# Forgetting attention rebuilt on transposed scores, with rounded high and low parts, inside a two-block kernel

## The reference, cut to what matters

```python
proj = einsum('bld,de->ble', rmsnorm(x), w_in)      # z_ssm, xbc, dt, q, k, v, f, z_att, g_ssm, g_att
log_f = log_sigmoid(f_raw + fgate_b)                # 16 heads
fcum = cumsum(log_f, axis=-1)
for blk in range(8):                                # 128 queries each, head width 64
    s = einsum('bhqd,bhkd->bhqk', q[q0:q1], k[:q1]) * 64 ** -0.5
    s = s + fcum[q0:q1, None] - fcum[None, :q1]
    s = where(kpos <= qpos, s, -inf)
    prob = softmax(s, axis=-1)
    o[q0:q1] = einsum('bhqk,bhkd->bhqd', prob, v[:q1])
y_att = o * silu(z_att)
merged = sigmoid(g_ssm) * (y_ssm @ w_branch_ssm) + sigmoid(g_att) * (y_att @ w_branch_att)
out = x + rmsnorm(merged @ w_out)
```

## Time and profile before

| what | value |
|---|---|
| runs shown | 3496.93 us median of 3 (3496.38 to 3499.29) |
| profiled execution, its time / its span | 3497.23 us / 3495.4 us |
| PE, DVE, ACT, POOL busy over the span | 86%, 60%, 39%, 9% |
[...]

### The profile page before, as it was taken

One profiled execution on the slowest core, in us unless ns is written; L12 is line 12 of the kernel. 1 busy time (PEld: TensorE's weight loads), 2 busy tenths in 40 slices (PEclk: granted clock), 3 DMA queues, 4 the chain that ended last, 5 costly groups with the idle time before them and its releaser, 6 DMA issues. The chain is left out here.

```text
span 3495.4 us, 39550 instructions
## 1 busy us (share of the span) xinstructions
PE 2989.5 (86%) x14122; PEld 2406.6 (69%) x14122; DVE 2101.0 (60%) x2553; ACT 1376.2 (39%) x1961; POOL 298.9 (9%) x215
## 2 busy tenths in 40 slices
PE   6977886999988999998967994978799859999992
PEld 5855665888876777786756871656587848888881
DVE  4773544343325666334544789878345469999993
ACT  3342333323332333332243342333332237777770
POOL 0001300000000000000000000000000014443430
PEclk9986898999998999999988996989899769999996
DMA  3100010111221110111121110000111449999995
GB/s 85 49 14 1 0 43 24 48 49 49 97 78 38 25 25 13 49 49 37 43 72 44 49 32 0 1 25 25 43 49 43 172 153 394 383 376 375 376 351 225
DMA packets 169958, 349.60 MB, mean 100 GB/s; under 512 B 33313, under 2 KB 33313, under 8 KB 169824
## 3 DMA queue, kind: packets, MB, share of 16 engines
q1 hardware_dynamic: 158496, 322.66, 27.0%
q0 software_dynamic: 9216, 16.80, 1.3%
q10 hardware_dynamic: 2112, 8.39, 0.7%
HBM read 326.76 MB, written 37.81 MB: 104 GB/s over the span
## 5 line engine op out<-in xcount | busy, mean ns | idle before, releaser
L2069 DVE TENSOR_TENSOR ex_w<-ex_raw,ex_w 128x2048 fp32r<-128x2048 f32 x192 | 436.1, 2290 | 49.6 <-ACT ex_w L2016 47.2
L2016 ACT ACTIVATE ex_w<-ex_raw 128x2048 fp32r<-128x2048 f32 x192 | 364.0, 1916 | 89.9 <-DMA ex_raw<-in_w_down_e 32.4
L1946 PE MATMUL ps<-ex_w,ex_xT 128*128 128x512 f32 x1536 | 366.2, 395 | 5.3 <-DVE ex_xT L2078 5.1
L1946 PEld LDWEIGHTS ps<-ex_w,ex_xT 128*128 128x128 f32 x1536 | 287.2, 189 | 67.5 <-DVE ex_xT L2078 6.4
L729 DVE TENSOR_TENSOR bs_t<-arena,bs_t 128x1024 fp32r<-128x1024 f32 x80 | 98.1, 1226 | 283.3 <-ACT bs_t L693 283.3
L609 DVE SCALAR_TENSOR_TENSOR arena<-arena,small 128x1023 f32<-128x1023 f32 (+9 forms) x168 | 213.7, 1272 | 4.3
L672 PE MATMUL ps<-bs_t,bs_w 128*128 128x512 f32 x512 | 201.4, 393 | 11.1 <-DVE bs_w L732 9.0
L693 ACT ACTIVATE bs_t<-arena 128x1024 fp32r<-128x1024 f32 x80 | 84.9, 1061 | 298.2 <-PE ps L674 269.4
L673 PE MATMUL ps<-bs_t,bs_w 128*128 128x512 f32 x512 | 200.5, 392 | 0.0
L674 PE MATMUL ps<-bs_t,bs_w 128*128 128x512 f32 x512 | 200.4, 391 | 0.0
L1946 PE MATMUL ps<-ex_w,ex_hT 128*128 128x512 f32 x768 | 186.0, 399 | 7.3 <-DVE ex_hT L2089 7.3
(11 more groups left out here) (369 smaller groups left out, 6832.0 us busy)
## 6 DMA issues: line engine op xcount, KB each, us to landing
ex_raw<-in_w_gate_e SPq DMA_DIRECT2D x64, 1024.0 KB, 13.2
ex_raw<-in_w_up_e SPq DMA_DIRECT2D x64, 1024.0 KB, 13.1
ex_raw<-in_w_down_e SPq DMA_DIRECT2D x64, 1024.0 KB, 13.5
arena<-in_w_in SPq DMA_DIRECT2D x108, 512.0 KB, 3.7
arena<-in_x SPq DMA_DIRECT2D x4, 2048.0 KB, 11.5
arena<-in_w_out SPq DMA_DIRECT2D x16, 512.0 KB, 3.7
arena<-expert_out SPq DMA_DIRECT2D x8, 1024.0 KB, 12.2
arena<-in_w_branch_ssm SPq DMA_DIRECT2D x8, 512.0 KB, 3.7
```

The costliest lines, as they stand in the source:

```text
L1946: mm = nc.tensor.matmul(out, l, r, start=(k == 0 and n == 0), stop=(k == kc - 1 and n == 2))
L2016: nc.scalar.activation(half_of(part[m][0], h), raw[m][:, h * W // 2: (h + 1) * W // 2], ACT.Identity).then_inc(high[m], 1)
L2069: V.tensor_tensor(half_of(part[m][1], h), raw[m][:, h * W // 2: (h + 1) * W // 2], half_of(as_f32(part[m][0]), h), ALU.subtract)\
```

## The change

Scores are made transposed: keys in partitions, up to 512 queries in columns. A head has 12 tiles (g, j): 512 queries g by 128 keys j, cut at the diagonal to 512, 384, 256 or 128 columns, 4608 columns in all. All large products are fp32r.

- q, k and v leave the dense phase as high and low parts (kinds `split`, `split_T`): ACT rounds each bank into one tile, DVE subtracts into another, and ACT issues 8 DMAs for each q or k job and 2 for each v job, into DRAM tensors of packed rows: `qa`, `ka` (128 rows) and `qb`, `kb` (66 and 67 rows). The v jobs now come last.
- Per head PE makes a first approximation of the scores in the old orientation, only for the row maxima (`top`, L1032, L1035); DVE reduces them (L1166); PE turns the 128x8 maxima, ACT rounds them, and SP sends them to DRAM and back as one row of `b` (L959, L962).
- Per tile: two products make the score (L1060, L1062, mask L1065), ACT makes the exponential and a rounded copy, GpSimd subtracts for the low part, and PE makes three products with the values (L1084 to L1089). Ones stand beside the 64 columns of values, so that the sum of a column of probabilities comes out in another row of the same bank.
- The sums go to DRAM and back as 128x8 (L967, L969), are inverted, go to DRAM and back spread over 64 partitions (L974, L979), and DVE multiplies a pair of heads by them (L1185).
- The output is feature-major, so "ya" goes away; `za` and `ba` become one phase of eight jobs, with the gate multiplied on DVE beside the g_att jobs (`gate_heads`).
- `phase_decays` rounds the sums in two more DVE instructions, stores two rows, and fills rows of ones.

```diff
@@ phase_decays
+    run_high, run_low = (r[0:HEADS, :] for r in c.rounded("dec_run", 5, 2 * SEQ + 112, SEQ))
+    unit = c.ones[0:HEADS, :].unsqueeze(1).to_broadcast([HEADS, SEQ // P, P])
+            for t, row in (("qa", HD), ("qa", HD + 1), ("kb", HD + 2)):
+                sp.dma_start(att[t][:, row, :].rearrange("h (k n) -> h k n", n=P), unit)\
+                    .then_inc(stored, 16)
             sp.wait_ge(step, RUN_DONE)
-            sp.dma_start(fcum_dram, run).then_inc(stored, 16)
-            sp.wait_ge(stored, 16)
+            for row, part in ((HD, run_high), (HD + 1, run_low)):
-            st.done(V.tensor_tensor_scan(run, one_row, fT, 0.0, ALU.mult, ALU.add))
+            st.then_wait(V.tensor_tensor_scan(run, one_row, fT, 0.0, ALU.mult, ALU.add))
+            st.then_wait(V.tensor_copy(run_high, run))
+            st.done(V.tensor_tensor(run_low, run, run_high.bitcast(F32), ALU.subtract))
...
@@ phase_dense
+            def high_evict(j):
+                for m in splits:
+                    if m < j and jobs[m][3] is jobs[j][3]:
+                        act.wait_ge(kept[m], stores[m])
+                for t in range(TT):
+                    act.wait_ge(product, TT * j + t + 1)
+                    nc.scalar.activation(jobs[j][3][0][:, t * BANK:(t + 1) * BANK], c.ps[:, t, :],
+                                         ACT.Identity, scale=jobs[j][6]).then_inc(halved, 1)
+                for m in splits:
+                    if n - 1 == last[m] + 1 or (n == NS and last[m] >= NS - 1):
+                        if n == NS and last[m] >= NS - 1:
+                            high_evict(m)
+                        act.wait_ge(by_vec, before(m + 1, False))
+                        stores[m] = jobs[m][5](act, kept[m], jobs[m][3])
+                    elif j in splits:
+                        dve.wait_ge(halved, TT * splits.index(j) + t + 1)
+                        part = slice(t * BANK, (t + 1) * BANK)
+                        x = V.scalar_tensor_tensor(out=dst[1][:, part], in0=src, scalar=jobs[j][6],
+                                                   in1=dst[0][:, part].bitcast(F32), op0=ALU.mult,
+                                                   op1=ALU.subtract)
...
@@ phase_forget_attention, SP, GpSimd and PE of the new one
+            for h in range(HEADS):
+                if h + 2 < HEADS:
+                    load_a(h + 2)
+                if h + 1 < HEADS:
+                    load_b(h + 1)
+                if h:
+                    keep_sums(h - 1)
+                if h + 1 < HEADS:
+                    move_shift(h + 1)
+                if h % 2 == 0 and h + 2 < HEADS:
+                    load_v(h // 2 + 1)
+                if h:
+                    spread_inverse(h - 1)
...
+                    pool.wait_ge(rounded, x + 1)
+                    if x >= 4:
+                        pool.wait_ge(valued, x - 3)
+                    nc.gpsimd.tensor_tensor(low[x % 4][:, 0:w], prob[x % 3][:, 0:w],
+                                            f32(high[x % 4][:, 0:w]), ALU.subtract).then_inc(lowered, 1)
...
+                    pe.wait_ge(b_in[h % 2], 32 * (h // 2 + 1))
+                    pe.wait_ge(shift_in, 16 * (h + 1))
+                if x >= 3:
+                    pe.wait_ge(exped, x - 2)
+                bank = c.ps[:, S_BANK[x % 3], :]
+                (qa, ka), (qb, kb) = a_of[h % 3], b_of[h % 2]
+                diag = j >= 4 * g
+                nc.tensor.matmul(bank[:, 0:w], ka[:, ks], qa[:, qs], start=True, stop=False,
+                                 skip_group_check=True)
+                mm = nc.tensor.matmul(bank[:, 0:w], kb[0:BR, ks], qb[0:BR, qs], start=False,
+                                      stop=not diag, skip_group_check=True)
+                if diag:
+                    mm = nc.tensor.matmul(bank[:, 0:P], c.identb[:], c.maskTb[:, 0, :], start=False,
+                                          stop=True, skip_group_check=True)
...
+                pe.wait_ge(rounded, x + 1)
+                nc.tensor.matmul(to, vl_, high[x % 4][:, 0:w], start=(j == 0), stop=False,
+                                 skip_group_check=True)
+                nc.tensor.matmul(to, vh_, high[x % 4][:, 0:w], start=False, stop=False,
+                                 skip_group_check=True)
+                pe.wait_ge(lowered, x + 1)
+                nc.tensor.matmul(to, vh_, low[x % 4][:, 0:w], start=False, stop=(j == 4 * g + 3),
+                                 skip_group_check=True).then_inc(valued, 1)
+                    score(h, i)
+                    if h + 1 < HEADS and i < TT - EARLY:
+                        top(h + 1, i + EARLY)
+                    if h + 1 < HEADS and i == TT - EARLY + 1:
+                        turn_shift(h + 1)
+                    if h + 2 < HEADS and i >= NT - EARLY:
+                        top(h + 2, i - (NT - EARLY))
+                    if i >= 3:
+                        values(h, i - 3)
...
@@ phase_forget_attention, DVE of the new one
+                if h >= 3 and h % 2:
+                    norm((h - 3) // 2)
+                for t in range(EARLY, TT):
+                    if h + 1 < HEADS:
+                        maxima(h + 1, t)
+                if h:
+                    take(h - 1, 1)
+                take(h, 0)
+                if h:
+                    invert(h - 1)
+                for t in range(EARLY):
+                    if h + 2 < HEADS:
+                        maxima(h + 2, t)
+            take(HEADS - 1, 1)
+            invert(HEADS - 1)
...
@@ _build
+                    + [(T(R(0)), wcol(w_in, (C_Q, C_K)[n // 2], n % 2), "split_T", staged[n % 2], None,
+                        store_heads(n % 2, n // 2), (float(HD) ** -0.5, 1.0)[n // 2]) for n in range(4)]
+                    + [(T(R(0)), wcol(w_in, C_V, n), "split", staged[n % 2], None, store_values(n), 1.0)
+                       for n in range(2)], 5)
+        phase_forget_attention(c, att, sums, inverse, shifts)
+        def gate_heads(n, tapped, by_act, by_vec, moved):
+
+            for x in range(2 * (n - 2 * KC), 2 * (n - 2 * KC) + 2):
+                if 0 <= x < KC:
+                    if x == 0:
+                        nc.vector.wait_ge(by_act, 2 * TT)
+                    yk = T(R(4))[:, x, :]
+                    nc.vector.tensor_tensor(yk, yk, T(R(1))[:, x, :], ALU.mult).then_inc(tapped, 1)
+
+        phase_dense(c, "za", [(T(R(0)), wcol(w_in, C_ZA, n), "act_T", wide(1, n), ACT.Silu)
                               for n in range(2)]
                     + [(T(R(0)), wcol(w_in, C_GA, n), "act_T", wide(3, n), ACT.Sigmoid)
-                       for n in range(2)], 5)
-        phase_turn(c, "ya", R(4), R(5), gate=R(1))
-        phase_dense(c, "ba", [(T(R(5)), wcol(a["w_branch_att"][0], 0, n), "muladd_T", wide(2, n),
-                               wide(3, n)) for n in range(2)]
+                       for n in range(2)]
+                    + [(T(R(4)), wcol(a["w_branch_att"][0], 0, n), "muladd_T", wide(2, n),
+                        wide(3, n)) for n in range(2)]
                     + [(T(R(2)), wcol(a["w_out"][0], 0, n), "act", half(R(3), n), ACT.Identity)
-                       for n in range(2)], 1, made_by={2: 0, 3: 0})
+                       for n in range(2)], 5, aside=gate_heads, made_by={6: 4, 7: 4}, gated_by=(4, 5))
```

More of the change, by code:

```diff
@@ new lines, in phase_forget_attention @@
+    NT = 3 * TT // 2
+    TILES = [(g, j) for g in range(2) for j in range(4 * g + 4)]
+    assert len(TILES) == NT
+    BR, EARLY = HD + 3, 5
+    a_of = [c.named(f"fa_a{s}", 1, s * 2 * SEQ, SEQ, F32R, 2) for s in range(3)]
+    b_of = [c.named(f"fa_b{s}", 3, s * 2 * SEQ, SEQ, F32R, 2) for s in range(2)]
+    rinv = [c.named(f"fa_rinv{s}", 1, 6 * SEQ + s * SEQ, SEQ) for s in range(2)]
+    prob = [c.named(f"fa_p{s}", 3, 4 * SEQ + s * BANK, BANK) for s in range(3)]
+    high = [c.named(f"fa_ph{s}", 3, 4 * SEQ + (3 + s) * BANK, BANK, F32R) for s in range(4)]
@@ new lines, in phase_forget_attention @@
+    shift = c.named("fa_shift", 3, 4 * SEQ + 7 * BANK, 2 * P, F32R)
+    VW = 3 * HD
+    vh, vl = ([c.named(f"fa_v{n}{s}", 5, (2 * s + n) * TT * VW, TT * VW, F32R)
+               .rearrange("p (t n) -> p t n", t=TT) for s in range(2)] for n in range(2))
+    low = [c.named(f"fa_pl{s}", 5, 4 * TT * VW + s * BANK, BANK, F32R) for s in range(4)]
+    out = c.at(4, 0, REGION)
+    negmax = [c.small[:, SEQ + TT * s:SEQ + TT * (s + 1)] for s in range(2)]
+    inv = [c.small[:, SEQ + 16 + TT * s:SEQ + 16 + TT * (s + 1)] for s in range(2)]
@@ L899, in phase_forget_attention @@
-        turned = S("turned")
-        placed = S("placed")
-        summed = S("summed")
-        stored = S("stored")
+        a_in, b_in = [S(f"a_in{s}") for s in range(3)], [S(f"b_in{s}") for s in range(2)]
+        v_in = [S(f"v_in{s}") for s in range(2)]
+        filled = S("filled")
+        topped, negated = S("topped"), S("negated")
+        shift_turned, shifted = S("shift_turned"), S("shifted")
```

(80 more changed lines are left out.)

349 lines of the change are left out of this document (197 added, 152 removed).

## The result

The changed kernel takes 3710.57 us (median of four runs, 3687.82 to 3711.99) against 3496.65 for the kernel before on the same chip: ratio 1.0604, interval 1.0565 to 1.0642. I had forecast 3452 us and faster; it is 214 us slower.

The account below looks back on a forecast made before the run. The prediction took TensorE to bound the attention stage, at about 348 us. From 3497.2 us it subtracted 22.3 (attention and its earlier start) and 25.4 (joined phases) and added 2.5 (`phase_decays`): 3452 us, range 3404 to 3492.

Parts of the forecast that it names:

- the pricing of the dense phases: In `bs`, the added stores and their issues cost nothing; up to 8 us allowed in the range.
- rival C: In the attention, SP's small hops take 4.5 us instead of 1.9 behind loads: 3525 us, slower than before; chance 0.08.
- start of bs: Before the dense phase, two more operations in `phase_decays` on the path to the store add 2.5 us.
- to the attention: Between `bs` and the attention, the first product comes 2.3 us earlier, with the clearing gone from the path.
- attention: From the attention's first product to `za`: 328.5 us against 348.5 before, 20 less.
- za and ba joined: Joining the two phases removes TensorE's gap between them except a 0.3 us boundary: 25.4 us less.
- The late inverse: In odd heads, the inverse returns late behind value loads: 5.4 us lost in each of 7 pairs, 38 us.
- The start of the attention: Eight blocks of maxima, turn, rounding and the way out and back put the first score 14 us after the first product.
- A head: One attention head takes 16.6 us: 14.8 of TensorE products and masks, plus 0.5, 0.8 and 0.5.
- rival B: In the attention, narrow products and slower tile hand-overs make a head 18.4 us: 3481 us; chance 0.17.
- Narrow products: Twelve 128-column products a head cost between 0.117 us and 0.234 us (two records) each; 0.5 us a head taken.
- what would show it wrong: Attention signs: odd and even heads equal, `shift_in` ending TensorE's wait, ACT mostly waiting for GpSimd, or heads under 15.5 us.

Follow-up runs that it names:

- e9: Only groups of stores from ScalarE's queue, back to back, the rest of the computation left out; the four 62-row stores took 83.7 us together.
- e1: The changed kernel with only its 62-row stores cut into 48 and 14 rows: 3585.96 us, ratio to the kernel before 1.0254.
- e5: e3 with the stores of a query or key job issued in pairs behind five steps of the next job: 3453.09 us, ratio to the kernel before 0.9879.
- e4: Only loads of different row counts, the rest of the computation left out: 64 rows took 3.5 us, 62 took 7.5, 67 took 12.6.
- e2: The changed kernel with only the 67- and 66-row loads of `b` cut into 64 rows and a rest: 3649.62 us, ratio to the kernel before 1.0434.
- e3: The changed kernel with both the store cut of e1 and the load cut of e2: 3520.13 us, ratio to the kernel before 1.0073.
- e6: e3 with VectorE's product with the inverse moved later in odd heads, behind takes and reciprocal: 3490.37 us, ratio to the kernel before 0.9994.
- e7: e3 with the edits of e5 and e6 together: 3429.7 us, ratio to the kernel before 0.9808.

## Why the prediction was wrong

**The step that failed** is the pricing of the dense phases: "The 8 issues of 0.38 us a job fit into ACT's free 3.9 us of a step. Cost: nothing", with up to 8 us allowed in the range. It measured 184 us. The 0.38 us came from an issue of before, which stored all 128 rows and had an empty queue. Neither held for the new stores. One pair of the stores of each job has 62 rows and ran on two engines (share 0.13 in after, and 0.12 over e9's four such stores; 124 us, e1), and eight DMAs with 6 MB stand in a row on one queue, where ScalarE was held at its issues still when the shape was right (19.4 us a job in e1, none in e5: 62 us). I had only asked how long the bytes take on all engines. I had also asked whether weight loads are held up, and not whether ScalarE itself comes back.

**The row count, second place.** I had the `b` loads of 66 and 67 rows at the rate of the large ones. With one engine for `att_kb` (share 0.06 in after, and for 67 rows in e4) the small store behind it took 7.7 us instead of 1.9: 61 us (e2). This is rival C's mechanism in part (hops behind the loads of the next heads, forecast from 1.9 to 4.5 us each), which I gave 0.08 because "the loads are issued at the head's start and need 4 us". Not the bytes ahead of the hop but the one engine that works on them made it slow: cut into 64 rows and a rest (e3), the same bytes leave the hop at 1.2 us, so C's reason is false. Its path was another one too: in after TensorE waited only once, for 1.0 us, for the row of maxima, and 69.6 us for reductions, which stood behind DVE's waits for the sums and for the inverse. Its outcome would have come even so: with `bs` at nothing the other rows of the table still make after 24.6 us slower than before.

**What held.** With both shapes right and the issues spread, which is the kernel that my sum described, e5 takes 3453.09 us; the sum said 3452. That these agree to 1 us is luck: e5's runs lie between 3442.73 and 3464.13, its profiled execution is 35.3 us below that of before (3461.89 against 3497.23) where the sum had 45.2, and the attention gave 8.2 us of the 20. By its parts:

| part | forecast | e5 against before |
|---|---|---|
| start of bs | +2.5 | +3.2 |
| bs | 0 | -1.2 |
| to the attention | -2.3 | -4.2 |
| attention | -20 | -8.2 |
| za and ba joined | -25.4 | -27.4 |

- The start: `phase_decays` cost what I said.
- The joined phases: right (362.8 us against 389.6), including the gate's products between the steps.
- The late inverse: forecast 5.4 us in each of 7 odd heads, 38 in all. The wait measured 31.8 in e3; its removal gave 23.3 us (e6) and, beside the spread stores, 30.0 (e7, 315.9 us against 345.9). The place, the number of times and the sign were right. Part of the gain is the clock: TensorE's busy time falls from 283.3 (e5) to 269.6 us (e7) for the same 1424 instructions, as the granted clock rises from 0.88 to 0.95.
- The start of the attention: forecast 14 us from first product to first score, measured 16.7 in e7. I had taken the maxima at the product times of before, read where the granted clock is 1.00 (1033.8 to 1036.8 us), and they ran at 0.50.
- A head: 16.6 us forecast. In e7 the first score starts at 1075.8 and the last value product at 1358.7, 17.7 us a head, where I had 264 us for the whole. That is 1.1 of the 1.8 us a head that rival B added, though not for the first of its two reasons, as the last point shows; its second, slower hand-overs, I have not tested. So 19 us of e7's attention are my heads, and e7 is at 3430 instead of 3414. TensorE was busy 258.6 us of these 283, 16.2 a head, against the 14.8 of products that I counted, and 16.5 us of waits for the maxima (20 times) are 1.0 a head where I had 0.5. GpSimd's subtraction took 1.278 us for 512 columns in after, not the 1.04 of the earlier trace rows, but TensorE waited for it only 5.8 us in all. The 1.4 us by which the busy time is above my count I have not split further; the record of a product is longer than the distance to the next one (0.28 us against 0.11 and 0.12 in the lines below).
- Narrow products: fp32r products of 128 columns start 0.11 to 0.12 us apart, each with one record, not two; the first reason of rival B is excluded. In after:

```profile
1411.65 0.28 PE L1086 MATMUL ps<-fa_ph,fa_v 128*128 128x128 f32 x1
1411.76 0.28 PE L1089 MATMUL ps<-fa_pl,fa_v 128*128 128x128 f32 x1
1411.88 0.28 PE L1060 MATMUL ps<-fa_a 128*128 128x128 f32 x1
```

My claim of what would show it wrong was too narrow: it looked only at the attention, and none of its signs could fire in bs. The chance of 0.90 for faster took for granted that `bs` costs nothing, which I had argued only from the bytes on all engines and from the length of one issue.

## What to carry to other kernels

Look at the leading size of every DMA that a change adds, before its bytes: 62 or 67 rows of 4 KB took 7.5 and 12.6 us where 64 took 3.5, at DMA shares of 0.12 and 0.06, which is 2 and 1 of 16 engines (e4), and cutting them into 48 + 14 or 64 + 3 costs one more issue. ScalarE, which computes and also issues DMAs, stood 50.6 us at the issues of one job in after and 19.4 in e1, so a burst of megabytes belongs in pieces between its steps, as in e5. The price of an issue read from an empty queue says nothing of a later one in a row: in after the sixth of a job took 20.9 us.

## What the runs showed of the hardware

- Stores from 64 partitions (pieces of 4 KB) moved at 197 GB/s, from 128 partitions (pieces of 2 KB) at 392. These are the stretches of the first two groups of e9 (no engine computes: POOL, clock, DMA share, GB/s):

```profile
8.60:30.00 21.40, 0.00 (x0) 1.00 0.95 197
...
51.10:72.50 21.40, 0.00 (x0) 1.00 0.95 392
```

The share of busy time is the same in both, so it doesn't tell the rate. Why the one moves at half the speed of the other is not shown: the partitions and the size of the pieces changed together.

- In `bs` the held issues cost more than TensorE's waits for them; the clock granted afterwards added to it. The four waits of TensorE in `bs` are 176.0 us, the phase lost 184.2; after the stall shown above a dozen products start 0.43 us apart instead of 0.227, an estimated 2.4 us. Between 870 and 925 us of after, the granted clock is 0.90 in the mean.
